# Hymba-style hybrid layer on 8 cores: q and k of the retention heads transposed by DMA, a dense state product, and another order of the weight loads

## The chip, the cores and the metric

The kernel runs on the 8 cores of one Trainium2 chip, one program on all of them with different data. The metric is device time in microseconds (us) of the slowest core. TensorE (PE) does the matrix products and can transpose through the identity; VectorE (DVE), ScalarE (ACT) and GpSimd (POOL) do the elementwise work; SyncE (SP) issues every DMA of this kernel, loads, stores and transposes, in one order.

## The reference, cut to what matters

One layer: RMSNorm, one input projection split in eight, an attention branch with a sliding window of 128 keys (8 query heads, 2 key heads of 64), a retention branch (4 heads, q and k of 64, v of 128), a SiLU gate on each, one output projection, the residual, a last RMSNorm. BATCH is 4, SEQ 8192, D_MODEL 1024. The retention part, which the change touches:

```python
q = rotate_pairs(q, cos, sin)
k = rotate_pairs(k, cos, sin) * (RET_QK_DIM ** -0.5)
...
sc = jnp.einsum('bnchd,bnmhd->bnhcm', q, k) * decay_in[None, None]
o_inner = jnp.einsum('bnhcm,bnmhe->bnche', sc, v)
kv_chunk = jnp.einsum('bnmhd,bnmhe,hm->bnhde', k, v, k_dec).astype(jnp.float32)
def step(state, kv):
    return state * chunk_decay[None, :, None, None] + kv, state
_, prev = lax.scan(step, init, jnp.moveaxis(kv_chunk, 1, 0))
...
o_cross = jnp.einsum('bnchd,bnhde,hc->bnche', q, prev, q_dec)
```

## The kernel before, in words

**Split.** Each core computes one half of one sequence: 32 main chunks of 128 tokens (32 to 63; `NP` is 32). Ahead of them it runs 32 prefix chunks (0 to 31), which only build the retention state that the half starts from. (For a first half they are zeros; the work is the same.)

**Prefix chunk.** x is loaded (512 KB, 7 slots `xs`), its norm computed (ACT squares and sums, L680, POOL takes the power, L683) and the rows scaled to `hh` (L524 on ACT or L526 on DVE). PE transposes `hh` (`st_T`, 8 matmuls, L701), DVE or ACT copies the result to `hT`, PE multiplies by the k columns of the weights (`st_P_prefix`, L708, 8 matmuls of 256 columns), DVE rotates a pair of chunks (`ev_rot`, L740, L743 and two adds), and PE adds k times `hh` to four banks (`st_G`, L948, 4 matmuls of 512 columns). In the same stretch the weights come in: `load_wr` loads 16 pieces of 640 KB through three staging slots `wstage`, and ACT and DVE cast them to bf16 in `Wa` (v, key, value, q and k columns) and `Wb` (attention q and the two gates). A piece of part 0 holds `Wa`'s columns and a first quarter of attention q's, one of part 1 the rest of `Wb`. Then `load_wo` brings the output weights, 8 pieces of 512 KB. A piece can be loaded only when the cast of the piece three before it is done.

**Main chunk.** `st_P_main` part 1 projects attention q, k and v, retention q and k (rotated to `qk` by `ev_rot`, four slots) and v; part 2 (`P2`) the two gates. `st_R` transposes `qk` on PE (4 transposes) into a bank and copies it out in three pieces, `kT` and two zero-padded `qTp`, padded so that two heads share a 128-row product. `st_SC` and `st_scT` make the two kinds of scores, `st_PV`, `st_OR` and `st_KV` the outputs and the new state `Sst`, `st_M` transposes the mixed output by DMA, `st_O` multiplies by the output weights `Wo`, adds x and norms, `st_store` stores.

**Order.** The stages are laid out over steps t by the list `order`: an entry ("name", offset in the prefix, offset in the main part) runs chunk t - offset. In a step of the main part the stages come as T (chunk t+1), load (t+3), tload (t+4), M (t-2), store (t-4), PV, OR and KV (t-1), O (t-3), R (t), SC (t), P (t+1), scT (t), P2 (t+1), front (t+3). PE and SP run strictly in this order. ACT, DVE and POOL get theirs from a planner (`Sched.schedule`) that simulates the five engines with estimated costs, 310 GB/s for DMA among them, and picks at each moment the most urgent ready operation; some copies may go to either of two engines. On the chip every engine then runs its list in order, with semaphores between them. Small constants go by `emit_late_consts` at step NP - 12, the 512 KB of final gains `fg_rep` with them, all on one semaphore that is waited for in full.

## Time and profile before

| | |
|---|---|
| time of 3 runs | median 671.64 us (670.05 to 704.31) |
| profiled execution | 673.29 us; its span on the slowest core 671.7 us |
| spans of the 8 cores | 661.8 to 671.7 us, granted clock 0.965 to 0.980 |
| PE busy | 607.1 us, 90% |
| DVE busy | 525.8 us, 78% |
| ACT busy | 414.8 us, 62% |
| POOL busy | 204.3 us, 30% |
| DMA | 50.4% of 16 engines' span, 94.14 MB |

The profile shows the slowest core. The time of an execution is 1.6 us more than that core's span. Busy shares are means over two parts: the prefix with the weight loads, until some 124 us, and the main chunks behind it. A slice's granted clock of 1.00 is TensorE at its 2.4 GHz level. In a timeline the duration of a row of PE has the filling of the array in it, so that the distance of two starts, and not a duration, says what an instruction costs.

### The profile page before, as it was taken

What the parts mean: (1) busy time and instruction counts of PE and PEld (TensorE: products, weight loads), DVE (VectorE), ACT (ScalarE), POOL (GpSimd) and SP (SyncE); (2) the same over time, 40 slices, a digit from 0 to 9 for tenths busy, and PEclk for the clock granted to TensorE, in tenths of its full rate; (3) what the DMA queues carried; (4) which work ended last, traced back from release to release, by engine and by line L of the source; (5) the groups of instructions that cost most, each with busy time, mean ns of one, the idle gap of its engine ahead of it and who ended that gap; (6) DMA issues with size and microseconds to landing.
All of it is one profiled execution on the core that took longest, in us unless ns stands there. A gap on an engine that the chain in (4) does not pass through costs nothing.

```text
span 671.7 us, 19097 instructions; the slowest of 8 cores (661.8 to 671.7 us)
## 1 busy us (share of the span) xinstructions
PE 607.1 (90%) x5059; PEld 372.0 (55%) x5059; DVE 525.8 (78%) x1047; ACT 414.8 (62%) x732; POOL 204.3 (30%) x264
## 2 busy tenths in 40 slices
PE   0697869797899999999999999999999999999974
PEld 0464646555555555566555556566555655555541
DVE  0687877556678888888888888788888888888874
ACT  4776877564446756766666567666676675665532
POOL 2644432212212323322322322323333332332230
PEclk9997879798899999999999999999999999999978
DMA  7999997723324444535625446637356353414113
GB/s 191 337 311 337 325 307 226 248 64 80 80 64 111 110 113 126 131 77 133 135 65 159 111 99 124 128 95 131 101 130 147 101 132 101 112 49 111 49 48 110
DMA packets 89337, 94.14 MB, mean 140 GB/s; under 512 B 68624, under 2 KB 69008, under 8 KB 89232
## 3 DMA queue, kind: packets, MB, share of 16 engines
q1 hardware_dynamic: 89232, 92.93, 50.4%
q8 instruction: 43, 0.70, 0.4%
q14 instruction: 62, 0.51, 0.3%
HBM read 59.88 MB, written 16.78 MB: 114 GB/s over the span
## 4 chain that ended last, share of the span: by engine, by line
PE 78%; DMA 5%; issue 5%; DVE 5%; ACT 4%; POOL 2%; SPq 1%; DVEq 0%; POOLq 0%; ACTq 0%
PE ps L708 34%; PE ps L1018 16%; PE ps L714 11%; PE ps L871 4%; PE ps L948 2%; PE ps L904 2%; DMA dkt<-dk_pre 2%; DMA fg_rep_s<-fg_rep 2%; PE ps L701 1%; DMA wstage<-w_o 1%; PE ps L994 1%; PE ps L990 1%; ACT PT L874 1%; PE ps L929 1%; PE ps L849 1%
## 5 line engine op out<-in xcount | busy, mean ns | idle before, releaser
L708 PE MATMUL ps<-Wa,hT 128*128 128x512 bf16 (+2 forms) x1032 | 169.5, 319 | 2.2 <-DVE hT L512 2.2
L708 PEld LDWEIGHTS ps<-Wa,hT 128*128 128x128 bf16 x1032 | 89.8, 100 | 59.9 <-issue 2.6
L708 PE MATMUL ps<-Wb,hT 128*128 128x512 bf16 x512 | 115.7, 379 | 1.9 <-ACT sqk L771 1.9
L1018 PE MATMUL ps<-Wo,mixT 128*128 128x512 bf16 x512 | 116.0, 380 | 0.0
L880 POOL TENSOR_SCALAR_AFFINE_SELECT PT<-PT 128x1024 bf16<-128x1024 bf16 x63 | 81.2, 1301 | 52.3 <-ACT PT L874 52.3
L1001 POOL TENSOR_TENSOR gns<-gns,neghalf 128x4 f32<-128x4 f32 x32 | 33.0, 1031 | 174.8 <-DVE gns L999 174.7
L1018 PEld LDWEIGHTS ps<-Wo,mixT 128*128 128x128 bf16 x512 | 50.3, 98 | 54.6 <-issue 1.0
L708 PEld LDWEIGHTS ps<-Wb,hT 128*128 128x128 bf16 x512 | 48.5, 98 | 56.1 <-issue 2.9
L874 ACT ACTIVATE PT<-ps,negC 128x1024 bf16<-128x1024 f32 x64 | 71.1, 1113 | 4.3 <-DVE negC L782 3.8
L680 ACT ACTIVATE junk<-xs 128x1025 bf16<-128x1025 f32 x64 | 67.5, 1055 | 2.7 <-DMA xs<-x_all 1.3
L714 PEld LDWEIGHTS ps<-hT,Wb 128*128 128x128 bf16 x1024 | 63.9, 102 | 5.7 <-issue 2.5
L714 PE MATMUL ps<-hT,Wb 128*128 128x128 bf16 x1024 | 66.7, 227 | 0.0
L683 POOL TENSOR_TENSOR stat<-stat,neghalf 128x1 f32<-128x1 f32 x64 | 41.6, 659 | 79.6 <-ACT junk L680 76.6
L510 ACT ACTIVATE kT<-ps 128x256 bf16<-128x256 bf16 x31 | 11.9, 383 | 85.6 <-PE ps L849 85.6
L831 ACT ACTIVATE gate<-ps 128x512 f32<-128x512 f32 x64 | 38.2, 596 | 42.9 <-PE ps L708 17.0
L834 DVE SCALAR_TENSOR_TENSOR gate<-gate,ps 128x512 f32<-128x512 f32 x64 | 43.8, 685 | 12.7 <-ACT gate L831 10.8
L1029 POOL TENSOR_TENSOR stat<-stat,neghalf 128x1 f32<-128x1 f32 x32 | 17.6, 550 | 112.2 <-ACT junk L1027 112.2
L1022 DVE TENSOR_TENSOR yy<-ps,xs 128x512 f32<-128x512 f32 x64 | 44.2, 691 | 4.7 <-PE ps L1018 1.6
L1031 DVE SCALAR_TENSOR_TENSOR yy<-yy,stat,fg_rep_s 128x1024 f32<-128x1024 f32 x32 | 40.9, 1277 | 7.9 <-POOL stat L1029 7.7
L871 PE MATMUL ps<-aqT,kTa 128*128 128x512 bf16 x128 | 35.5, 381 | 8.4 <-DVE Sst L937 4.7
L1027 ACT ACTIVATE junk<-yy 128x1025 bf16<-128x1025 f32 x32 | 33.9, 1060 | 13.9 <-DVE yy L1022 10.2
L740 DVE TENSOR_TENSOR rotu<-ps,tb 128x512 f32<-128x512 f32 x48 | 33.0, 687 | 6.7 <-PE ps L708 5.5
(126 smaller groups left out, 1009.3 us busy)
## 6 DMA issues: line engine op xcount, KB each, us to landing
xs<-x_all SPq DMA_DIRECT2D x64, 512.0 KB, 8.3
out<-yy SPq DMA_DIRECT2D x32, 512.0 KB, 3.1
wstage<-w_r SPq DMA_DIRECT2D x16, 640.0 KB, 11.5
tb<-tabs SPq DMA_DIRECT2D x32, 256.0 KB, 4.6
wstage<-w_o SPq DMA_DIRECT2D x8, 512.0 KB, 7.1
wstage<-w_k SPq DMA_DIRECT2D x2, 512.0 KB, 6.6
gate<-cs_pre SPq DMA_DIRECT2D x2, 512.0 KB, 13.0
fg_rep_s<-fg_rep SPq DMA_DIRECT2D x1, 512.0 KB, 11.5
```

The costliest lines, as they stand in the source:

```text
L680: S.add("act", lambda e: e.activation(out=junk[:, 0:D + 1], in_=xs[sx][:, 0:D + 1], func=AF.Square, accum_out=stat[st][:, 0:1]), reads=[b_ ...
L683: S.add("pool", lambda e: e.tensor_tensor(out=stat[st][:, 2:3], in0=stat[st][:, 0:1], in1=neghalf[:, 0:1], op=ALU.pow), reads=[b_stat[st], ...
L708: S.add("pe", lambda e, kb=kb: e.matmul(bank[:, c0:c0 + n], lhsT=hT[c % 2][:, kb * 128:(kb + 1) * 128], rhs=W[:, kb, w0:w0 + n], start=(kb ...
L714: S.add("pe", lambda e, kb=kb: e.matmul(bank[:, c0:c0 + 128], lhsT=W[:, kb, w0:w0 + 128], rhs=hT[c % 2][:, kb * 128:(kb + 1) * 128], start ...
L831: S.add("act", lambda e, bank=bank, gi=gi: e.activation(out=gate[s2][:, gi * 512:(gi + 1) * 512], in_=bank[:, 0:512], func=AF.Tanh, scale= ...
L834: S.add("dve", lambda e, bank=bank, gi=gi: e.scalar_tensor_tensor(out=gate[s2][:, gi * 512:(gi + 1) * 512], in0=gate[s2][:, gi * 512:(gi + ...
L871: S.add("pe", lambda e, bank=bank, sk=sk, g=g, first=first: e.matmul(bank[:, g * 512:(g + 1) * 512], lhsT=kTa[sk][g][:], rhs=aqT[s2][:], s ...
L874: S.add("act", lambda e, blk=blk, bank=bank: e.activation(out=PT[s2][blk][:], in_=bank, func=AF.Exp, bias=negC[s2][:, 0:1], scale=ATT_SCAL ...
L880: S.add("pool", lambda e, blk=blk, sgn=sgn, op=op: e.affine_select(out=PT[s2][blk][:], in_=PT[s2][blk][:], pattern=[[0, 8], [-sgn, 128]], ...
L1018: S.add("pe", lambda e, kb=kb, bank=bank, half=half: e.matmul(bank[:, 0:512], lhsT=mixT[s2][:, kb * 128:(kb + 1) * 128], rhs=Wo[:, kb, hal ...
L1022: S.add("dve", lambda e, bank=bank, half=half: e.tensor_tensor(out=yy[s2][:, half * 512:(half + 1) * 512], in0=bank[:, 0:512], in1=xs[sx][ ...
L1031: S.add("dve", lambda e: e.scalar_tensor_tensor(out=yy[s2][:, 0:D], in0=yy[s2][:, 0:D], scalar=st[:, 2:3], in1=fg_rep[:], op0=ALU.mult, op ...
```

## The change

Retention q and k are rotated straight into a zero-padded tile `qkp` of 8 blocks of 128 columns (two slots; in the prefix into the buffers `PT[1]`), and one DMA transpose makes all of `qkT` from it. The transposes on PE and the three copies are gone, and stage R moves ahead of M in the order. The state product takes the padded k: four products of 128 columns, accumulated in pairs, in place of two of 256, and the state is updated by two fused DVE operations in place of one multiply and two adds. `load_wr` loads 8 pieces of 640 KB, one per step `-4 + 22 i // 7`; the rest of attention q comes as two pieces of 512 KB at steps 19 and 21, the gates' columns as eight pieces of 512 KB at steps 24 to 31 with buffers of their own (`b_Wg`), the output weights four each at steps 32 and 33 (before: one each at steps 26 to 33), the constants at step 25 (before 20), and `fg_rep` by itself at step 34. The last x that the prefix's part of the order loads (chunk 33) is at step 24, chunk c at step c - 9.

```diff
-    order=[("T", None, -1), ("load", -9, -3), ("tload", -3, -4), ("M", None, 2), ("store", None, 4), ("GF", 2, None),
-           ("PV", None, 1), ("OR", None, 1), ("KV", None, 1), ("O", None, 3), ("G", 1, None), ("R", None, 0), ("SC", None, 0),
+    order=[("T", None, -1), ("load", -9, -3), ("tload", -3, -4), ("R", None, 0), ("M", None, 2), ("store", None, 4), ("GF", 2, None),
+           ("PV", None, 1), ("OR", None, 1), ("KV", None, 1), ("O", None, 3), ("G", 1, None), ("SC", None, 0),
...
+    qkp_all = sb("qkp", [128, 2 * 1024 + 128], BF16)
+    qkp = [qkp_all[:, i * 1024:(i + 1) * 1024] for i in range(2)]
+    qkT, b_qkT = slots("qkT", 2, [128, 8, 128], BF16)
+    qk_pre = [PT[1][i // 2][:, (i % 2) * 512:(i % 2 + 1) * 512] for i in range(4)]
...
+    S.add("pool", lambda e: e.memset(qkp_all[:], 0.0), writes=b_qk)
...
+    def emit_fg():
+        S.add("sp", dma(fg_rep[:, :], fg_d[:, :]), writes=[b_fgs], dmaq="fg")
...
+    def load_wq(half):
+        st_t, b_st, q = stage_slot()
+        S.add("sp", dma(st_t[:, 0:1024], wq_d[:, half * 1024:(half + 1) * 1024]), writes=[b_st], dmaq=q)
+        for i in range(4):
+            kb = half * 4 + i
+            cast(Wb[:, kb, 256:512], st_t[:, i * 256:(i + 1) * 256], g_col[:, kb:kb + 1], b_st, b_Wb[kb])
+    def load_wg(kb):
+        st_t, b_st, q = stage_slot()
+        S.add("sp", dma(st_t[:, 0:D], wg_d[kb * 128:(kb + 1) * 128, :]), writes=[b_st], dmaq=q)
+        cast(Wb[:, kb, 512:WB], st_t[:, 0:D], g_col[:, kb:kb + 1], b_st, b_Wg[kb])
...
-            cast(Wb[:, kb, 256:WB], st_t[:, :], col, b_st, b_Wb[kb])
...
-    for i in range(16):
-        w_tasks.setdefault(min(-4 + (30 * i) // 15, -4 + (i * (NP - 2)) // 15), []).append(
-            lambda i=i: load_wr(i // 2, i % 2))
     for i in range(8):
-        w_tasks.setdefault(NP - 6 + i, []).append(lambda i=i: load_wo(i))
+        task(-4 + (i * (NP - 10)) // 7, load_wr, i)
+    for i in range(2):
+        task(NP - 13 + 2 * i, load_wq, i)
+    for i in range(8):
+        task(NP - 8 + i, load_wg, i)
+    for i in range(8):
+        task(NP + i // 4, load_wo, i)
...
     def st_R(c):
-        for j in range(4):
-            S.add("pe", lambda e, j=j: e.transpose(pb[:, j * 128:(j + 1) * 128], qk[c % 4][:, j * 128:(j + 1) * 128],
-                                                   ident_bf[:]),
-                  reads=[b_qk[c % 4], b_const], writes=[bb])
-        S.add(cp(kT[s2][:].rearrange("p a b -> p (a b)"), pb[:, 256:512]), reads=[bb], writes=[b_kT[s2]])
-        for r in range(2):
-            S.add(cp(qTp[s2][r][r * 64:(r + 1) * 64, :, :].rearrange("p a b -> p (a b)"),
-                     pb[r * 64:(r + 1) * 64, 0:256]),
-                  reads=[bb], writes=[b_qTp[s2]])
+        S.add("sp", lambda e: e.dma_start_transpose(out=qkT[c % 2][:], in_=qkp[c % 2]),
+              reads=[b_qk[c % 2]], writes=[b_qkT[c % 2]], dmaq=f"tq{c % 2}", cost={"sp": 1.25, "dma": 4.0})
...
     def st_KV(c):
         for j in range(2):
-            S.add("pe", lambda e, j=j: e.matmul(bank[:, j * 256:(j + 1) * 256],
-                                                lhsT=qk[c % 4][:, 256 + j * 128:256 + (j + 1) * 128], rhs=rvv[:, j],
-                                                start=True, stop=True),
+            for r in range(2):
+                q = r * 2 + j
+                S.add("pe", lambda e, j=j, r=r, q=q: e.matmul(
+                    bank[:, j * 128:(j + 1) * 128], lhsT=qkp[c % 2][:, r * 512 + (2 + j) * 128:r * 512 + (3 + j) * 128],
+                    rhs=rv[c % 3][:, q * 128:(q + 1) * 128], start=(r == 0), stop=(r == 1)),
...
-        S.add(tt(Sst[:].rearrange("p a b -> p (a b)"), Sst[:].rearrange("p a b -> p (a b)"), cdtab[:], ALU.mult),
-        for r in range(2):
-            S.add("dve", lambda e, r=r: e.tensor_tensor(out=Sst[r * 64:(r + 1) * 64, :, :],
+        for j in range(2):
+            S.add("dve", lambda e, j=j: e.scalar_tensor_tensor(
+                out=Sst[:, j, :], in0=Sst[:, j, :], scalar=cdtab[:, j * 128:j * 128 + 1], in1=bank[:, j * 128:(j + 1) * 128],
+                op0=ALU.mult, op1=ALU.add), reads=[bb, b_S, b_constB], writes=[b_S])
...
-        if t == max(0, NP - 12):
+        if t == max(0, NP - 7):
             emit_late_consts()
+        if t == NP + 2:
+            emit_fg()
```

## Rows read from the trace of the kernel before

**Rows 1.** Busy time by stretch: start:end, length, PE, PEld, DVE, ACT, POOL, clock, DMA share, GB/s.

```profile
50.00:85.00 35.00, 28.53 (x220) 19.31 (x218) 29.12 (x51) 25.58 (x41) 16.06 (x23) 0.85 1.00 328
85.00:118.00 33.00, 26.21 (x216) 18.45 (x216) 24.43 (x48) 24.66 (x33) 10.46 (x16) 0.90 0.81 268
320.00:400.00 80.00, 79.46 (x683) 47.65 (x682) 67.59 (x142) 51.83 (x95) 24.33 (x25) 1.00 0.43 107
```

**Rows 2.** Timeline of PE in the prefix: start, us, line, operation, count, idle before.

```profile
15.39 1.01 PE L701 MATMUL ps<-ident_bf_s,hh 128*128 128x128 bf16 x8 [15.39 <-DVE hh L526]
...
68.45 0.61 PE L701 MATMUL ps<-ident_bf_s,hh 128*128 128x128 bf16 x8
...
70.64 0.61 PE L701 MATMUL ps<-ident_bf_s,PT 128*128 128x128 bf16 x8
...
93.52 1.01 PE L701 MATMUL ps<-ident_bf_s,hh 128*128 128x128 bf16 x8 [4.08 <-DVE hh L526]
...
115.25 0.61 PE L701 MATMUL ps<-ident_bf_s,hh 128*128 128x128 bf16 x8 [1.25 <-DVE hh L526]
...
121.43 0.27 PE L765 MATMUL ps<-sqk,ones_bf 128*128 128x128 bf16 x1 [3.65 <-ACT sqk L771]
...
124.06 3.16 PE L714 MATMUL ps<-hT,Wb 128*128 128x128 bf16 x32
```

**Rows 3.** Timeline of SP's DMA issues at the prefix's end.

```profile
93.46 1.82 SPq L497 DMA_DIRECT2D xs<-x_all  x2
...
100.53 9.91 SPq L497 DMA_DIRECT2D wstage<-w_o  x3
...
122.62 0.33 SPq L497 DMA_DIRECT2D wstage<-w_o  x1
```

**Rows 4.** Costliest groups by shape: count, busy us, mean ns, idle before it.

```profile
L510 ACT ACTIVATE qTp<-ps 64x256 bf16<-64x256 bf16 x60 | 22.7, 378 | 5.3 <-ACT qTp L510 0.7
L937 DVE TENSOR_TENSOR Sst<-Sst,ps 64x256 f32<-64x256 f32 x64 | 26.5, 415 | 2.6 <-DVE Sst L937 0.5
L512 DVE CAST kTa<-ps 64x128 bf16<-64x128 f32 x51 | 14.6, 286 | 16.9 <-PE ps L708 13.7 <-ACT kTa L510 1.9
```

**Rows 5.** Timeline of PE over two main chunks.

```profile
323.50 1.95 PE L714 MATMUL ps<-hT,Wb 128*128 128x128 bf16 x32
...
330.51 3.61 PE L708 MATMUL ps<-Wb,hT 128*128 128x512 bf16 x16 [0.27 <-ACT sqk L771]
...
339.70 1.95 PE L714 MATMUL ps<-hT,Wb 128*128 128x128 bf16 x32
...
350.72 0.38 PE L929 MATMUL ps<-rv,qk 128*128 128x256 bf16 x2
350.94 3.62 PE L1018 MATMUL ps<-Wo,mixT 128*128 128x512 bf16 x16
354.39 0.39 PE L849 MATMUL ps<-ident_bf_s,qk 128*128 128x128 bf16 x4
354.62 1.03 PE L871 MATMUL ps<-aqT,kTa 128*128 128x512 bf16 x4
355.48 1.95 PE L714 MATMUL ps<-hT,Wb 128*128 128x128 bf16 x32
...
361.83 0.39 PE L890 MATMUL ps<-qTp,kT 128*128 128x128 bf16 x4
```

**Rows 6.** What PE waited for from 200 to 600 us: total us, times, longest.

```profile
PE ps L708 <- ACT sqk L771: 1.9, 7, 0.3
```

**Rows 7.** Timeline of DVE: the second rotation add of a main chunk.

```profile
349.57 0.42 DVE L517 TENSOR_TENSOR qk<-rotw,rotu 128x256 bf16<-128x256 f32 x1
```

**Rows 8.** Timeline of SP: the transpose of the mixed output behind it.

```profile
351.53 1.22 SPq L691 DMA_TRANSPOSE mixT<-mix  x1
```

**Rows 9.** The transposes into `mixT`, from issue to landing.

```profile
DMA to landing us min/median/max: 3.0/3.4/6.0
```

**Rows 10.** DMA issues: tiles, queue, count, KB each, median us to landing.

```profile
wstage<-w_r SPq DMA_DIRECT2D x16, 640.0 KB, 11.5
```

95 lines of the change are left out of this document (47 added, 48 removed).

## The prediction

> **What bounds the kernel now.** I read the busy time by stretches first, then PE's and SP's timelines at the places where the stretches differ, then the groups by shape for durations, last the waits. From 320 to 400 us PE is busy for 79.46 of 80 us at the full clock, with DVE at 84% and ACT at 65% [rows 1]: the main chunks are bound by PE, and only what leaves PE's list shortens them. A chunk takes 15.78 us (339.70 to 355.48), or 16.20 where PE waits ahead of the gates (323.50 to 339.70) [rows 5].
>
> The prefix is another matter. PE is busy for 28.53 of 35 us from 50 to 85 us, at a clock of 0.85, while the 16 DMA engines are busy all the time at 328 GB/s [rows 1]. Counted from the transposes of chunk 0 at 15.39 us, those of chunk 32 come at 115.25, so that a chunk takes 3.12 us; where nothing is late it takes 2.19 (68.45 to 70.64) [rows 2]. So some 30 us of the prefix's 100 are not PE's work. Three candidates stand behind them: DMA, full until 85 us; DVE and ACT, together 103.8 us busy in the 68 us from 50 to 118, 76% of each [rows 1]; and single stalls, of which 93.52 (4.08 us idle) and 121.43 (3.65 us) are the largest [rows 2].
>
> **1. Fewer bytes ahead of the prefix's x.** By the order, and with 0.524 MB for a chunk of x or a 512 KB piece and 0.655 for 640 KB, what had to move before: x of chunks 0 to 30, 16.3 MB; 14 pieces of w_r, 9.2; k columns and tables, 2.2; constants with the gains, 1.05. That is 28.7 MB, 88 us at 0.328 MB per us [rows 1], behind some 3 us of start: 91 us, and SP does issue the next x at 93.46 [rows 3]. After the change: 16.3 of x, 8 pieces, 5.2, k columns and tables 2.2, the two pieces of attention q 1.05: 24.8 MB, 76 us, so 79. DMA brings the prefix's x 12 us earlier. Chunk 32 followed that issue by 22 us in the trace (93.46 to 115.25), since seven slots of x lie between; I keep this lag. The other bounds of this term: if DVE and ACT set the pace, it is almost nothing, since nearly all of their work stays (the gates' casts only move; two output weights' casts and the gains' scaling, about 3 us of ACT, leave). At two engines fully busy, their 103.8 us over 68 and a like share before need about 76 us for what takes 101 now, and PE needs 15.4 + 32 x 2.19 = 85.5 us at least: the gain cannot pass 22 us. I take 12, and 1 more for the 4.08 us stall, which ends a wait of DVE and POOL for the constants with the 512 KB of gains: the gains go by themselves now, but a wait for the rest stays. **-13 us**, ends -3 and -22.
>
> **2. The gap ahead of the first main chunk.** PE waits 3.65 us until 121.43 for ACT's square of the key [rows 2]; ACT there sits behind output weights that SP issues from 100.53 to 122.62 [rows 3]. They go away, but the gates' weights come to ACT just before in their place. **-2 us**, ends 0 and -3.65.
>
> **3. The gates' weights.** Eight pieces from step 24. Cumulated up to the last one: 24.8 MB, three more x, 1.6, eight pieces, 4.2, constants and tables, 1.6: 32.2 MB, 98 us, 101 with the start. Part 2 of chunk 32 needs them all. Part 2 starts 7 us behind part 1 (323.50 to 330.51) [rows 5]; with items 1 and 2 part 1 of chunk 32 starts at 109 in place of 124.06 [rows 2], part 2 at 116. So they are hidden by 15 us if DMA is the limit; cost 0. If they come at the pace of the output weights, one per 3.2 us (8 in 22 us, [rows 3]), issued from step 24 (about 84 us, where the x's of item 1 end) on, the last is issued at 107 and cast by 114: still hidden, by 2 us. This cover is thin, and it is a rival below.
>
> **4. Output weights and gains in the main part.** 4.7 MB at steps 32 to 34, first needed by O of chunk 32 three steps after. DMA is busy 43% in main chunks [rows 1], and 14 us of full DMA spread over some 50 us fit. But SP's list is strict: the transposes for chunks 33 (R) and 34 (hT) stand behind them, and casts of 1 to 2 us fall on ACT and POOL in the chunks that start the pipeline. **+1 us**, ends 0 and +4.
>
> **5. Four transposes less on PE.** From the first to the next instruction 0.23 us (354.39 to 354.62) [rows 5] for 32 chunks: **-7 us**. This is exact as long as PE is the bound; the lower end is -5, if the first and last chunks don't give it. The state product stays equal: two of 256 columns take 0.22 us (350.72 to 350.94), and four of 128 also take 0.22, as the four transposes show. The longer list of weight loads is hidden under the products, as now.
>
> **6. Relief of ACT and DVE.** ACT loses three copies of 0.38 us, 1.1 us per chunk; DVE loses the multiply and two adds (0.41 + 2 x 0.415, [rows 4]) and gets two fused operations on 128 x 128 from PSUM. The trace has none of these; a cast from PSUM of 128 columns takes 0.286, a 256-column add 0.415 [rows 4], and I take 0.29, the row of the same width: 1.24 less 0.58, so 0.66 us less per chunk. Neither engine is the bound; what it can return is the wait for ACT's sqk ahead of the gates, 7 times from 200 to 600 us [rows 6], each of which goes with a chunk of 16.20 instead of 15.78. Between 0 and -3 us: **-1.5**. The rotation's adds write the same number of elements in another stride: 0, ends 0 and +0.1 us of DVE a chunk, hidden. The one fill of `qkp` on POOL, some 2 us, lies in the start, where POOL waits.
>
> **7. R as a DMA transpose.** Its issue holds SP for 1.22 us as `mixT`'s does [rows 8], and it lands 3.0 to 6.0 us after, median 3.4 [rows 9]. It waits for the second rotation add, at 349.57 + 0.42 = 350.0 [rows 7]; its reader, the product of q and k, starts at 361.83 [rows 5]. 11.8 us against 3.4: hidden by 8. Queued behind R on SP are M (here issued at 351.53 [rows 8], so at most 1.3 us later, and its reader O one full chunk behind), the store, and the next step's T, load and tload, each read half a chunk or more later. DMA's share rises from 0.43 by some 0.1: x, tables and output are 1.31 MB a chunk, 4.0 us at the full rate, 0.25 of it, so that the two transposes now fill the other 0.18 and one more is 0.09. Cost 0, and what it costs if the cover goes is the rival below.
>
> On this point the Trainium skill speaks against the change: "VectorE: DVE Perf Modes", in its rules for kernel authors, says to transpose 128 x 128 on TensorE where a PSUM destination is fine, and by DMA otherwise; in "The three transpose paths" it gives 390 ns against 1309 ns. By an estimate from this page eight blocks one behind the other would take 10.5 us; that would still end at about 360.5, 1.3 us ahead of the reader, and the sum would be the same by a hair. The trace's 3.4 us for an equal tile decides it here.
>
> **Sum.** -13 - 2 + 0 + 1 - 7 - 1.5 + 0 = -22.5 us. The profiled execution takes 673.3 us (span 671.7), so 650.8; it lies 1.7 above the median of the runs, so **649 us** against 671.6. About 2% (13.4 us) is what a measurement of this kernel can tell from no change.
>
> **Rivals.** (a) The prefix doesn't speed up: DVE, ACT and the planner's order set its pace, for which it speaks that chunk 32 comes 22 us behind the issue of its x. Against it: both stand at 76%. Then -3 for item 1, and -1 - 7 - 1 of the rest: 660 us. Chance 0.17. (b) The gates' weights come late: three staging slots, casts in ACT's list, 2 us of cover. Late by 6 us, PE idles, and its clock falls as in the stretches with gaps (0.85 and 0.90 [rows 1]): 6 us and 1 for the clock, 656 us. Chance 0.13. (c) Slower: the new wait in SP's queue, or R's landing, decides. A 640 KB load took 11.5 us to land in the full prefix [rows 10]. From the point where a transpose needs more than 11.8 us from the last rotation add, each us costs 32; at 13 us, with 1.2 over, +38 against -22: 687 us. For it: three transposes in one queue. Against it: the DMA share of 0.43. Chance 0.06. (d) The order by the planner comes out worse in the main chunks, with waits of 0.4 us in each: 660 us. Chance 0.06. My forecast: 0.58.
>
> Faster by over 2% (below 658.2): the forecast, most of (b), a fourth of (a) and (d): 0.75. Slower by over 2%: 0.05. Within: 0.20. The range reaches from the forecast with item 1 near its far end (-9 more), item 2 and 6 at theirs (-3), 637, to (a) and (d) with some more, 664.
>
> **What would show it.** The transposes of chunk 32 near 102 us and PE's first main product near 109; DMA at full share for less than 80 us, then the gates' pieces until about 100; no transposes of `qk` on PE, chunks of 15.55 us, steady; `qkT` landing in 3 to 4 us and no wait of PE for it; DVE near 82% in main chunks. The forecast is wrong if chunk 32 stays near 112, if PE waits for a gate weight, or if main chunks stay at 15.8.

## The result and the profile after

The changed kernel takes 664.02 us (median of 4 runs, 662.81 to 664.97) against 671.96 for the kernel before beside it: a ratio of 0.989, with an interval of 0.987 to 0.992. The forecast was 649, range 637 to 664. The change is worth 8 us where 22.5 were expected; it is faster, by less than 2%. In some executions the cores of one die run several per cent slower (704.31 us in one of the four of the kernel before, more in a few below); every ratio and every range given here leaves those out. The profiled execution took 664.39 us, its span 662.8 on core 4.

The busy time by stretches comes first, as in [rows 1] (start:end, length, PE, PEld, DVE, ACT, POOL, granted clock, DMA share, GB/s):

```profile
50.00:85.00 35.00, 26.43 (x215) 18.23 (x213) 30.07 (x53) 28.44 (x48) 16.89 (x25) 0.90 0.95 318
85.00:118.00 33.00, 24.60 (x220) 17.32 (x219) 22.64 (x44) 24.55 (x34) 6.57 (x11) 0.90 0.89 276
320.00:400.00 80.00, 80.00 (x685) 47.63 (x684) 66.69 (x137) 48.41 (x85) 24.78 (x27) 1.00 0.55 146
```

The last line is the success: PE is busy 80.00 of 80 us, the waits of before are gone, and ACT and DVE have less to do. The first two hardly differ from before: PE is no busier between 50 and 118 us than it was (51.0 us against 54.7), though fewer bytes lie ahead of it. DMA's share is 0.95 where it was 1.00, and 0.89 where it was 0.81; DVE and ACT together are at 105.7 of 136 engine-microseconds.

PE's timeline in the prefix, the transposes of a chunk each (those of chunks 17, 18 and 32 are the rows at 63.65, 73.18 and 106.51):

```profile
15.02 1.01 PE L722 MATMUL ps<-ident_bf_s,hh 128*128 128x128 bf16 x8 [15.02 <-DVE hh L530]
...
63.65 0.61 PE L722 MATMUL ps<-ident_bf_s,hh 128*128 128x128 bf16 x8
...
69.81 1.86 PE L729 MATMUL ps<-Wa,hT 128*128 128x256 bf16 x8 [5.55 <-DVE hT L516]
...
73.18 1.06 PE L722 MATMUL ps<-ident_bf_s,PT 128*128 128x128 bf16 x8
...
102.14 0.61 PE L722 MATMUL ps<-ident_bf_s,mix 128*128 128x128 bf16 x8 [0.89 <-DVE mix L530]
...
106.51 0.61 PE L722 MATMUL ps<-ident_bf_s,hh 128*128 128x128 bf16 x8
...
116.19 0.27 PE L796 MATMUL ps<-sqk,ones_bf 128*128 128x128 bf16 x1 [7.30 <-ACT sqk L802]
```

Chunk 32 comes at 106.51 instead of 115.25 [rows 2], 8.7 us earlier, not 13. And the wait for ACT's square of the key, 3.65 us before, is now 7.30. The key is that of chunk 31, the last of the prefix, which the first main chunk's window needs; so this wait falls between the transposes of chunk 32 and its first product.

PE's timeline of a main chunk:

```profile
330.67 1.95 PE L735 MATMUL ps<-hT,Wb 128*128 128x128 bf16 x32
...
337.02 0.39 PE L911 MATMUL ps<-qkT 128*128 128x128 bf16 x4
...
341.69 0.39 PE L951 MATMUL ps<-rv,qkp 128*128 128x128 bf16 x4
341.91 3.62 PE L1035 MATMUL ps<-Wo,mixT 128*128 128x512 bf16 x16
345.36 1.03 PE L892 MATMUL ps<-aqT,kTa 128*128 128x512 bf16 x4
346.23 1.95 PE L735 MATMUL ps<-hT,Wb 128*128 128x128 bf16 x32
```

Start to start it is 346.23 - 330.67 = 15.56 us, against 15.78 in [rows 5]. The transposes ahead of L892 are gone, and the state product takes the 0.22 us (341.69 to 341.91) that were expected of four products of 128 columns.

To place the difference I read five marks on each of the 8 cores and take medians: the transposes of chunk 32 (T32), the first products of chunks 32, 36 and 63 in the main part (P32, P36, P63), and the end of the span.

| us | T32 | P32 | P32 to P36 | P36 to P63 | P63 to end | end |
|---|---|---|---|---|---|---|
| before | 112.8 | 121.7 | 69.6 | 431.9 | 45.2 | 668.3 |
| after | 104.8 | 117.0 | 69.4 | 421.0 | 51.3 | 658.7 |
| difference | -8.0 | -4.7 | -0.2 | -10.9 | +6.1 | -9.6 |

A column is the difference of two medians. By the slowest cores the change is worth 671.7 less 662.8, 8.9 us, and by the medians of the runs 7.9. So the forecast's 22.5 went three ways: 10.3 us are missing in the prefix (-4.7 for -15), 6.1 were lost at the end, where nothing was expected, and the main part gave 3.6 more than the 7.5 that items 4 to 6 sum to. -22.5 + 10.3 + 6.1 - 3.6 = -9.7. The experiments are about these three.

**Where in the prefix the 8.0 us came.** The same medians for more chunks' transposes, with the half of the change that keeps the old loads (below) beside them:

| us | T17 | T18 | T23 | T24 | T25 | T32 |
|---|---|---|---|---|---|---|
| before | 66.6 | 68.8 | 85.5 | 92.0 | 96.2 | 112.8 |
| old loads, R by DMA and dense product | 63.3 | 65.4 | 80.2 | 91.5 | 95.5 | 111.9 |
| after | 63.2 | 72.1 | 84.3 | 86.5 | 88.7 | 104.8 |

At chunk 23 the change had gained 1.2 us. Between chunks 23 and 25 it gained 6.3 more, behind chunk 25 the last 0.5. What lies between chunks 23 and 25 in the kernel before is the 4.08 us stop at 93.52 [rows 2]. DVE and POOL stand there until the constants have landed, the 512 KB of gains with them (DVE, then POOL, core 1):

```profile
91.13 0.17 DVE L569 TENSOR_SCALAR sinks<-sinks_s 128x8 f32<-128x8 f32 x1 [1.32 <-DMA fg_rep_s<-fg_rep]
...
91.97 2.71 POOL L683 TENSOR_TENSOR stat<-stat,neghalf 128x1 f32<-128x1 f32 x4 [2.97 <-DVE negsinkmax L573]
```

POOL's four powers are those that the scaling of the next chunks' rows waits for. In the kernel of the table's second row the prefix has come further by then, the stop is longer, and chunk 24 comes at the same time (core 6, DVE and PE):

```profile
90.71 0.17 DVE L569 TENSOR_SCALAR sinks<-sinks_s 128x8 f32<-128x8 f32 x1 [6.78 <-DMA fg_rep_s<-fg_rep]
...
93.10 1.01 PE L701 MATMUL ps<-ident_bf_s,hh 128*128 128x128 bf16 x8 [9.82 <-DVE hh L528]
```

So in the old order of loads the landing of the constants pinned chunk 24, and most of the prefix's gain is that wait gone. Whether the gains by themselves, the later step or the fewer bytes ahead took it away, no run separates. Against it stands a new stop, the 5.55 us at 69.81 above: chunk 18 comes 3.3 us later than before.

### The profile page after: what moved, and what is told of

Same layout as the page of the kernel before. It is cut to its first block, busy times and chain, and to the rows that moved or that the text cites. A ratio compares the mean times of both kernels' runs of the same rounds, so it can differ in the third digit from the quotient of the medians.

```text
span 662.8 us, 18824 instructions; the slowest of 8 cores (655.3 to 662.8 us)
## 1 busy us (share of the span) xinstructions
PE 594.6 (90%) x4995; PEld 362.1 (55%) x4995; DVE 503.1 (76%) x1001; ACT 384.6 (58%) x657; POOL 201.0 (30%) x262
## 4 chain that ended last, share of the span: by engine, by line
PE 79%; DMA 9%; DVE 3%; ACT 3%; issue 3%; POOL 1%; SPq 1%; DVEq 0%; POOLq 0%; ACTq 0%
PE ps L729 36%; PE ps L1035 16%; PE ps L735 11%; DMA xs<-x_all 5%; PE ps L892 4%; PE ps L925 2%; DMA wstage<-w_g 2%; PE ps L965 2%; DMA wstage<-w_r 1%; PE ps L911 1%; PE ps L1007 1%; PE ps L1011 1%; PE ps L951 1%; PE ps L789 1%; ACT junk L701 1%
## 5 line engine op out<-in xcount | busy, mean ns | idle before, releaser
L729 PE MATMUL ps<-Wa,hT 128*128 128x512 bf16 (+2 forms) x1032 | 165.6, 314 | 9.2 <-DVE hT L516 8.0
L729 PEld LDWEIGHTS ps<-Wa,hT 128*128 128x128 bf16 x1032 | 87.8, 99 | 66.1 <-issue 9.9
L729 PE MATMUL ps<-Wb,hT 128*128 128x512 bf16 x512 | 117.2, 383 | 0.0
L901 POOL TENSOR_SCALAR_AFFINE_SELECT PT<-PT 128x1024 bf16<-128x1024 bf16 x63 | 77.3, 1236 | 62.8 <-ACT PT L895 62.7
L701 ACT ACTIVATE junk<-xs 128x1025 bf16<-128x1025 f32 x64 | 67.6, 1056 | 10.5 <-DMA xs<-x_all 5.7
L514 ACT ACTIVATE Sbfp<-Sst 128x256 bf16<-128x256 f32 x31 | 12.9, 417 | 73.5 <-DVE Sst L956 70.5
L865 DVE SCALAR_TENSOR_TENSOR gate<-gate,ps 128x512 f32<-128x512 f32 x64 | 43.7, 684 | 10.5 <-ACT gate L862 8.3
L892 PE MATMUL ps<-aqT,kTa 128*128 128x512 bf16 x128 | 35.1, 388 | 8.6 <-DVE Sst L956 4.3
## 6 DMA issues: line engine op xcount, KB each, us to landing
wstage<-w_r SPq DMA_DIRECT2D x8, 640.0 KB, 12.3
```

Source lines behind the costliest of these rows:

```text
L701: S.add("act", lambda e: e.activation(out=junk[:, 0:D + 1], in_=xs[sx][:, 0:D + 1], func=AF.Square, accum_out=stat[st][:, 0:1]), reads=[b_ ...
L729: S.add("pe", lambda e, kb=kb: e.matmul(bank[:, c0:c0 + n], lhsT=hT[c % 2][:, kb * 128:(kb + 1) * 128], rhs=W[:, kb, w0:w0 + n], start=(kb ...
L865: S.add("dve", lambda e, bank=bank, gi=gi: e.scalar_tensor_tensor(out=gate[s2][:, gi * 512:(gi + 1) * 512], in0=gate[s2][:, gi * 512:(gi + ...
L892: S.add("pe", lambda e, bank=bank, sk=sk, g=g, first=first: e.matmul(bank[:, g * 512:(g + 1) * 512], lhsT=kTa[sk][g][:], rhs=aqT[s2][:], s ...
L901: S.add("pool", lambda e, blk=blk, sgn=sgn, op=op: e.affine_select(out=PT[s2][blk][:], in_=PT[s2][blk][:], pattern=[[0, 8], [-sgn, 128]], ...
```

## The experiments

Each was timed beside the kernel before in the same job; "marks" are the medians over cores, as above. A ratio is against the kernel before.

### Each half alone

The weights' half alone (the order and form of the loads; transposes and state product as before):

```
 kernel before
-    for i in range(16):  w_tasks ... load_wr(i // 2, i % 2)
-        w_tasks.setdefault(NP - 6 + i, []).append(lambda i=i: load_wo(i))
+    for i in range(8):   task(-4 + (i * (NP - 10)) // 7, load_wr, i)
+    for i in range(2):   task(NP - 13 + 2 * i, load_wq, i)
+    for i in range(8):   task(NP - 8 + i, load_wg, i)
+        task(NP + i // 4, load_wo, i)
+        if t == NP + 2:  emit_fg()
...
```

> The kernel before with the changed weight loads alone; R on TensorE and the old state product stay. Marks are medians over the 8 cores: before, chunk 32's transposes at 112.8 us, first main product at 121.7, chunk 63's first product at 623.2, end 668.4; changed kernel 104.8, 117.0, 607.4, 658.8. Theory A (the parts add, the prefix's gain is the weights'): first main product at 117, then the old 501.5 us to chunk 63 and the old tail of 45.2: some 667 us. Rival B (the tail's loss of 6.3 us comes from the weights and gains, loaded later): tail 51, 673 us.

Measured: 677.21 us (674.93 to 678.5) against 671.37, ratio 1.008 (1.006 to 1.011): slower. T32 105.9, P32 117.7, P36 to P63 436.2, end part 46.4. The prefix is shorter by 4 us, as in the whole change, and P36 to P63 is longer by 4.3.

The other half alone (R as a DMA transpose, `qkp`, dense state product; loads as before):

```
 kernel before
-            S.add("pe", lambda e, j=j: e.transpose(pb[:, j * 128:(j + 1) * 128], qk[c % 4][...], ident_bf[:]), ...)
-        S.add(cp(kT[s2]...)) ; for r in range(2): S.add(cp(qTp[s2][r]...))
+        S.add("sp", lambda e: e.dma_start_transpose(out=qkT[c % 2][:], in_=qkp[c % 2]), ...)
-        S.add(tt(Sst, Sst, cdtab, ALU.mult)) ; for r in range(2): add of a 64x256 half
+        for j in range(2): scalar_tensor_tensor(Sst[:, j, :], cdtab, bank, mult, add)
...
```

> The changed kernel's DMA transposes of q and k and its dense state product, with the weight loads of before. Theory A (the parts add, the tail's loss belongs to this part): first main product at 121.7 as before, chunk 63 some 490 us later, tail 51 in place of 45: 667 us. Rival B (the tail's loss is from the weight loads): tail 45, 661 us.

Measured: 665.13 us (665.04 to 665.39), ratio 0.991 (0.988 to 0.993). T32 111.9, P32 121.7, P36 to P63 422.9, end part 50.0. So the prefix's gain is the weights' half's but for 0.9 us at T32, none of which is left at P32, and the main part's gain is wholly this one. The halves don't add: +5.8 and -6.2 us alone, -8 together. Where the weights' half lost its time is seen on core 4 of that kernel, in PE's timeline at the start of one of the last chunks:

```profile
602.74 0.38 PE L892 MATMUL ps<-aqT,kTa 128*128 128x512 bf16 x1 [0.95 <-DVE gg L1024]
...
606.05 0.38 PE L892 MATMUL ps<-aqT,kTa 128*128 128x512 bf16 x1 [2.94 <-DVE Sst L958]
```

The chunks there are 20.0 and 17.4 us apart; all those from chunk 36 to 61 are at 15.8 to 16.7. No weight is loaded any more at 600 us. PE's list is the same, instruction by instruction, as in the kernel before (5059 in both traces), and so is SP's from 150 us on. What differs is the lists of DVE, ACT and POOL that the planner wrote; the second half of the state's add stands on DVE behind the 1.28 us of the final norm's product and its wait.

### The end of the kernel: R's place

```
 changed kernel
-    order=[..., ("tload", -3, -4), ("R", None, 0), ("M", None, 2), ("store", None, 4), ("GF", 2, None),
+    order=[..., ("tload", -3, -4), ("M", None, 2), ("store", None, 4), ("R", None, 0), ("GF", 2, None),
```

> The changed kernel with one entry moved: stage R comes behind M and store in the order, in place of ahead of them. Theory A (ahead of M, R's place in SP's list hands its urgency to the rotation, and the shift of the attention's exponent, negC, falls behind it on DVE, which costs only where PE's list runs out): tail 46 to 47 us in place of 51.4, time 659 to 660. Rival C (the fused state update makes the tail longer): tail 51, time 664.

Measured: 659.49 us (658.51 to 661.29), ratio 0.982 (0.979 to 0.986), 4.5 us less than the change as it is. P32 117.5, P36 to P63 422.8, end part 45.3 in place of 51.3. What PE waited for from 600 us on (total us, times, longest), first the changed kernel, then this one:

```profile
PE ps L911 <- ACT PT L895: 4.7, 2, 2.4
PE ps L892 <- DVE Sst L956: 4.3, 1, 4.3
PE ps L925 <- POOL PT L901: 0.7, 1, 0.7
PE ps L1035 <- DMA mixT<-mix: 0.4, 1, 0.4
```

```profile
PE ps L911 <- ACT PT L895: 2.4, 1, 2.4
PE ps L892 <- DVE Sst L956: 2.2, 2, 1.7
PE ps L925 <- POOL PT L901: 0.7, 1, 0.7
```

One wait for the exponential, 2.24 us on core 4, is gone and that for the state is halved (the rows are of core 4 and of core 7, the slowest of each). The first of them begins far from PE. DVE in the changed kernel (start, us):

```profile
606.79 0.16 DVE L808 TENSOR_TENSOR tmpc<-Mk 128x1 f32<-128x1 f32 x1
...
618.15 0.15 DVE L811 TENSOR_TENSOR tmpc<-tmpc,Mq 128x1 f32<-128x1 f32 x1
...
618.68 0.27 DVE L813 TENSOR_SCALAR negC<-tmpc,cst,negsinkmax 128x1 f32<-128x1 f32 x1
```

The small operation that closes the softmax's bound stands 11 us behind its partner. What it reads had been there since 606.79; the list puts the final norm's product of a finished chunk (1.28 us) and the next chunk's rotation ahead of it. So ACT's exponential can start only at 619.10, and PE stands still at 620.36. After each such stop PE runs at the lower level for a while: from 612 to 640 us PE is busy for 18.39 of 28 us at a granted clock of 0.83 here, and for 22.65 at 0.88 with R behind. R's own data were in time: it landed 3.0 to 5.0 us after its issue, median 3.1, and PE never waited for it. R's place isn't the only edit that shortens the end. The runs below that change nothing but the prefix or the loads have an end part of 46.5 to 47.7 us too, so that the row of stops is shown as read in the trace, and R's place as its cause is not.

### The casts of the gates' weights allowed on POOL

```
 changed kernel
-        S.add(alts, reads=[st_buf, b_gs] + ([b_gnc] if gn else []), writes=[b_dst])
+        S.add(alts, reads=[st_buf, b_gs] + ([b_gnc] if gn is True else []), writes=[b_dst])
-        cast(Wb[:, kb, 512:WB], ..., b_Wg[kb])
+        cast(Wb[:, kb, 512:WB], ..., b_Wg[kb], "pool")
```

> The changed kernel with the casts of the gates' weights allowed on POOL beside ACT. Theory A (the 7 us wait ahead of the first main product is ACT, held in its list by casts that wait for the gates' loads): the stretch from chunk 32's transposes to the first main product falls from 12.3 us to 8 or 9, time 660 to 661. Rival D (the loads themselves set it): 12 us, time 664.

Measured: 656.58 us (656.01 to 656.92), ratio 0.978 (0.976 to 0.980). T32 105.1, P32 115.8: the gap is 10.7 us in place of 12.2, and not 8 or 9. The edit only allows POOL, and the planner sent two of the eight casts there:

```profile
L601 POOL TENSOR_TENSOR Wb<-wstage,g_col_s x2: 1892/1893/1894, 88.3 to 97.5; 128x1024 bf16<-128x1024 f32 x2
```

Six stayed on ACT, so the theory had a weak test. The end part is 47.6, 3.7 less, and that has no mechanism in this edit: its lists were planned anew. With R behind as well:

```
 changed kernel
+    both edits above
```

> Both edits that helped: R behind M and store, and the gates' casts on POOL or ACT. If they add: first main product at 116 us, tail 45, time 653 to 654. If wg_pool's shorter tail (47.6) was already the same gain as r_behind's: 655 to 656.

Measured: 657.23 us (656.06 to 657.52), ratio 0.978 (0.977 to 0.980): the same as the casts' edit alone. P32 115.6, end part 46.7. The two gains of the end part don't add.

### The fused update of the state

```
 changed kernel
+            S.add("dve", ... tensor_tensor(out=Sst, in0=Sst, in1=cdtab, op=ALU.mult))
-            ... scalar_tensor_tensor(out=Sst[:, j, :], ..., op0=ALU.mult, op1=ALU.add)
+            ... tensor_tensor(out=Sst[:, j, :], in0=Sst[:, j, :], in1=bank[...], op=ALU.add)
```

> The changed kernel with the state updated by a multiply and two adds of 128 columns in place of two fused operations; the dense product stays. DVE has some 0.4 us more per main chunk. Theory A (the tail's loss came with R's place): tail 50 to 52 us as in the changed kernel, main part 421, time 664 to 665. Theory C (the fused update made the tail longer): tail 46, time 659.

Measured: 663.06 us (661.45 to 663.43), ratio 0.986 (0.985 to 0.988); P36 to P63 421.2, end part 49.8. So the fusing as such is worth nothing that can be seen. In the changed kernel it takes

```profile
L956 DVE SCALAR_TENSOR_TENSOR Sst<-Sst,cdtab_s,ps x64: 293/340/349, 156.2 to 646.3; 128x128 f32<-128x128 f32 x64
```

340 ns in the median and not the 290 of my estimate.

### What limits the prefix

Three runs leave work out in the prefix. All three have their lists planned anew, and each is a single run. In the first the loads of five of the eight pieces of `w_r`, of `w_q` and of `w_g` are left out, the casts staying:

```
 changed kernel
-        S.add("sp", dma(st_t[:, 0:1024], wq_d[...]), ...)
-        S.add("sp", dma(st_t[:, 0:D], wg_d[...]), ...)
+        if kb < 3:
             S.add("sp", dma(st_t[:, :], wr_d[...]), ...)
```

> The changed kernel that leaves out the loads of five of the eight pieces of w_r, of the two of attention q and of the eight of the gates (8.5 MB); all their casts are still made, from what lies in the staging slots. Theory E (ACT and DVE): chunk 24's transposes at 84 to 86 us, chunk 32's at 103 to 105, first main product 5 us or more behind as the casts wait for nothing (110). Theory F (the loads): the 9 us step from chunk 17 to 18 falls to 3, chunk 24 at 78 to 80, chunk 32 at 96, first main product at 102 to 104.

In the second the prefix's squares go over 129 instead of 1025 columns:

```
 changed kernel
+        n0 = 0 if is_main(c) else 896
-        ... activation(out=junk[:, 0:D + 1], in_=xs[sx][:, 0:D + 1], func=AF.Square, ...
+        ... activation(out=junk[:, n0:D + 1], in_=xs[sx][:, n0:D + 1], func=AF.Square, scale=..., ...
```

> The changed kernel whose prefix chunks sum the squares over 128 columns of x (and the constant) in place of 1024: it leaves out 7/8 of that sum, some 0.8 us of ACT per prefix chunk. Marks as before, medians over the cores; changed kernel: transposes of chunk 17 at 63.1 us, of 18 at 72.1, of 24 at 86.5, of 32 at 104.8, first main product at 117.0. Theory E (ACT and DVE set the prefix's pace): chunk 24 some 8 us earlier, at 78, and chunk 32 at 96 to 99. Theory F (the loads' landing sets it, the full DMA): chunk 24 at 85 to 87, chunk 32 at 104.

And then both edits together:

> The changed kernel without the loads of five pieces of w_r, of w_q and of w_g (their casts stay and read what lies in the buffers), and with the prefix's squares taken over 129 of 1025 columns: both edits of the earlier runs nodma and cheap_sq together. Each alone left chunk 32's prefix transposes at 105 to 106 us. Theory A (the prefix after 50 us has two limits close to one another, the DMA engines with the in-order wait for their weights, and the work of ACT and DVE; each hides what the other one loses): together chunk 32's transposes are at 95 to 98, P32 at 106 to 109, the run 645 to 649 us. Theory B (neither of the two pins the prefix, but the chain per chunk, transposes, hT copy, products, rotation, state products, or DVE alone, which has 14 to 16 us of work in 20 in every variant): 102 or later, P32 at 112 or later.

| us | T18 | T24 | T25 | T28 | T30 | T32 | P32 | run |
|---|---|---|---|---|---|---|---|---|
| after | 72.1 | 86.5 | 88.7 | 95.3 | 100.5 | 104.8 | 117.0 | 664.02 |
| without the loads | 64.9 | 81.9 | 84.7 | 96.3 | 100.7 | 105.0 | 115.1 | 656.99 (one) |
| short squares | 61.1 | 81.2 | 83.5 | 90.1 | 100.2 | 105.0 | 115.2 | 655.24 (one) |
| both | 62.9 | 76.8 | 79.6 | 87.1 | 92.9 | 97.2 | 107.9 | 648.72 (one) |

Either edit alone brings chunks 18 and 24 forward by 5 to 11 us and chunk 32 not at all; both together bring chunk 32 forward by 7.6. That sum fits theory A of the third run; of the first two runs neither theory has both marks, T24 and T32. The busy times of core 0 from 65 to 85 us, without the loads, with the short squares, with both:

```profile
65.00:85.00 20.00, 16.53 (x143) 11.31 (x142) 19.55 (x36) 18.50 (x26) 9.51 (x13) 1.00 0.71 192
```

```profile
65.00:85.00 20.00, 16.16 (x131) 11.17 (x132) 17.43 (x31) 12.74 (x32) 10.47 (x16) 0.91 1.01 323
```

```profile
65.00:85.00 20.00, 18.59 (x169) 13.21 (x167) 19.70 (x39) 17.64 (x33) 9.57 (x13) 1.00 0.71 204
```

With the loads gone, DVE is busy 19.55 and ACT 18.50 of 20 us, with DMA at 0.71: this stretch is then bound by the two vector engines. With ACT relieved, DMA stands at its full share. With both lifted PE is busy 18.59 of 20.

The lead over the changed kernel is lost only behind these 20 us, and there no engine is full. Without the loads and with the short squares, core 0 from 85 us on:

```profile
85.00:105.00 20.00, 16.64 (x127) 11.50 (x126) 15.47 (x31) 17.63 (x26) 4.64 (x7) 0.83 0.29 82
```

```profile
85.00:105.00 20.00, 16.57 (x126) 11.54 (x125) 13.91 (x27) 11.90 (x18) 3.44 (x6) 0.83 0.84 277
```

Each has a stop of PE in it, with the granted clock at 0.83 over the stretch. Without the loads PE waits 3.36 us at 89.37 for a copy of `hT` that stands in ACT's list behind casts; the three chunks from 25 to 28 take 11.6 us. With the short squares it is the constants again, this time at step 25 (POOL, then PE):

```profile
93.95 2.71 POOL L705 TENSOR_TENSOR stat<-stat,neghalf 128x1 f32<-128x1 f32 x4 [8.77 <-DVE gn_col_s L579]
...
95.50 1.01 PE L723 MATMUL ps<-ident_bf_s,mix 128*128 128x128 bf16 x8 [3.43 <-DVE mix L530]
```

Every core has this stop, of 3.4 to 4.2 us, and the two chunks from 28 to 30 take 10.1 us; 5.2 us of lead end there. So that both edits together reach 97.2 and neither alone does is no proof of two limits of the whole prefix: one stop in each plan ate the lead. How much of the 7.6 us is the plan is open; `wo_late` below moves T32 by 6.8 us the other way with no edit to the prefix's work.

From the loads' side, SP's issue of the x of chunks 31 and 32 in the changed kernel:

```profile
81.30 2.89 SPq L501 DMA_DIRECT2D xs<-x_all  x2
```

In the kernel before, the x of chunk 31 was issued at 93.46 [rows 3]. That is 12.2 us earlier now, and the forecast's count of bytes gave 12, in part by luck: SP was waiting there not for the queue but for the slot of chunk 24's x, which came free only behind the stop for the constants (SP's longest wait between 80 and 96 us in the kernel before):

```profile
SPq L338 <- DVE hh L526: 7.3, 1, 7.3
```

The x before that, of chunk 30, was issued only 2.9 us earlier (82.23 to 79.32), that of chunk 32 11.1 (94.95 to 83.86). By landing they came 10.1 and 11.8 us earlier, so the transfers did gain about what the bytes say. It didn't help: in the changed kernel the x of chunk 32 landed at 89.75, and its transposes start at 106.51, 16.8 us later (13.7 in the kernel before). The lag from the issue of chunk 31's x to T32 grew from 21.8 to 25.2 us (81.30 to 106.51).

### The gap ahead of the first main product

The chain of the end goes through it like this in the changed kernel (start, us, what):

```profile
92.35 7.21 DMA wstage<-w_g
...
102.26 7.99 DMA wstage<-w_g
...
112.29 1.14 ACT Wb L600
...
114.48 0.84 issue
115.32 0.19 ACT junk L701
115.51 0.18 ACT Vaug L514
...
115.77 0.29 ACT sqk L802
```

Between 85 and 120 us 43.4% of the chain is the landing of gates' weights. The product that reads them is not what waits; ACT's list is, since their casts stand in it ahead of the square of chunk 31's key, which PE finished the products for at about 109 us. In the next run the gates' loads and casts are replaced by fills on POOL (the gates are then computed from zeros):

```
 changed kernel, load_wg(kb)
-        st_t, b_st, q = stage_slot()
-        S.add("sp", dma(st_t[:, 0:D], wg_d[...]), ...)
-        cast(Wb[:, kb, 512:WB], ...)
+        S.add("pool", lambda e: e.memset(Wb[:, kb, 512:WB], 0.0), writes=[b_Wg[kb]])
```

> The changed kernel with the eight loads and ACT casts of the gates' weights replaced by POOL memsets of the same tiles (the gates are then computed from zeros; the main part's instructions are all there). Theory A (the gates' loads and casts are what the prefix's end and the gap wait for, as the waits of ACT in front of sqk show): chunk 32's transposes are at 102 to 103 instead of 104.8, the gap to the first main product is 8 us instead of 12.2, P32 110 to 112. Theory B (the gap is the first main chunk's own chain and the output weights step into the place of the gates' weights): P32 stays at 115 to 117.

Measured: one run, 661.21 us. T32 106.9, P32 118.2, the gap 11.3: no gain at P32, and 0.9 us of the gap. ACT's waits from 95 to 120 us on core 0 hold this line,

```profile
ACT Wo L597 <- DMA wstage<-w_o: 2.5, 1, 2.5
```

and PE's wait for sqk is 5.5 us. The output weights, next in the list, have stepped into the place in part; ACT also waits 8.2 us for DVE, POOL and PE in these 25. So the chain above shows what held ACT in the changed kernel, and not that the gap would be shorter without it. (T18 is at 69.5, 2.6 earlier, yet T24 at 88.8, 2.3 later.) Moving those one chunk further, together with the casts allowed on POOL:

```
 changed kernel with the casts of the gates' weights allowed on POOL
-        task(NP + i // 4, load_wo, i)
+        task(NP + 1 + i // 4, load_wo, i)
```

> wg_pool (656.6 us) with the output weights' eight loads issued one chunk later. Theory A (in every variant the end of the prefix is pinned by ACT's list, in which casts that wait for whatever weights come last stand ahead of the squares of q and k of the first main chunk): the gap from chunk 32's transposes to its first product falls from 10.7 us to 7 to 8 us, P32 is 112 to 113, and the total 653 to 654 if the main part doesn't give it back. Theory B (the gap is the chain of the first main chunk itself, products, square, norm, rotation and transposes, with no previous chunk to fill it): P32 and the gap stay within 1 us, and the total at 656 to 658; if PE then waits for an output weight in chunk 32's last product, the start (P36 minus P32, 69.2) grows by 1 to 3.

Measured: 667.95 us (10 runs, 666.09 to 670.87), ratio 0.995 (0.993 to 0.997), 11 us slower than without the edit. T17 is already at 68.3 instead of 63.1, T32 at 111.9, P32 at 122.7, the gap 10.7: loads after chunk 32 were moved, and chunk 17 came 5 us later. The edit didn't test what it was meant to; the planner wrote another prefix, with all eight casts of the gates' weights on ACT. What the gap would be without output weights in it stays open.

### The planner's own figures

The planner orders the lists by costs that it is given. Four runs change one such figure and no stage; the order on DVE, ACT and POOL changes, and which of two engines makes a copy. The cost of a DMA transpose:

```
 changed kernel
-   cost={"sp": 1.25, "dma": 4.0}
+   cost={"sp": 1.23, "dma": 3.2}
```

> The changed kernel with one figure of the planner's cost model altered (a DMA transpose is costed at 1.23 us of SP's time and 3.2 us of landing instead of 1.25 and 4.0). The program issues the same instructions on the same data; PE's and SP's orders stay the same, and DVE's, ACT's and POOL's orders, and some choices between DVE and ACT, come out differently. Theory A (what the change was worth lies in its mechanisms, the planner's order being about as good either way): 664 us within 2. Theory B (differences of several us between variants, such as w_only's 5.8 us of loss and the 5 to 6 us by which R's place and the casts' engine shorten the tail, are mostly the planner's order of the vector engines in the main part and the tail): it differs from 664 us by 3 us or more, in main or tail, while the last prefix transposes stay at 105 and the first main product at 117.

Measured: 667.44 us (666.38 to 668.26), ratio 0.993 (0.992 to 0.995), 3.4 us slower than the change as it is. PE's and SP's lists are the same instructions in the same order. T32 104.5 and P32 116.5 stay, P36 to P63 421.2 stays; P32 to P36 is 73.7 instead of 69.4. A figure nearer to the measured 1.23 and 3.1 us made the start of the main part worse by 4.3 us, by the lists of DVE, ACT and POOL alone.

And the time from a load's end on the queue to its data:

```
 changed kernel with the casts of the gates' weights allowed on POOL
-                op.t1 = dma_free + 1.0
+                op.t1 = dma_free + 4.0
```

> wg_pool (the changed kernel with the casts of the gates' weights on POOL alone, 656.6 us) with the planner's assumed latency of a load raised from 1 to 4 us, so that DVE's and ACT's weight instructions stand later in their lists. Theory A (the 9 us step from chunk 17's to chunk 18's prefix transposes comes from DVE's list, in which the sum over the last piece of w_r stands ahead of chunk 17's hT copy and waits for a load that lands 9.6 us after its issue): the step shrinks to 5 us or less, chunk 24's transposes are at 82 to 84 instead of 86.5. Whether that reaches the first main product (115.8 in wg_pool) depends on the second wait, at ACT, for the gates' and the output weights: if that pins it, P32 stays at 115 to 116 and the total at 656 to 657; if the first stall counts, P32 is 112 and the total 652 to 653. Theory B (the DMA engines, busy 95%, are the limit of the prefix and the list only shows where it waits): nothing of the prefix moves by more than 1 us.

Measured: 653.53 us (653.19 to 654.63), ratio 0.973 (0.972 to 0.975), 3 us less than with the figure at 1 us, and the fastest that keeps the computation. One of the eight casts is on POOL here, not two and not all as the text above has it. And it wasn't by the way expected: the step from chunk 17 to 18 is still 8.3 us (64.1 to 72.4), T24 is at 87.5, later by 1, T32 at 106.2. DVE doesn't wait there for `w_r` any more and the copy of `hT` still stands behind its sum:

```profile
68.49 0.67 DVE L630 TENSOR_REDUCE vmean<-wstage 128x4 f32<-128x512 f32 x1
...
70.41 0.68 DVE L516 COPY hT<-ps 128x1024 bf16<-128x1024 bf16 x1
```

so there the place in the list, not the load, makes the stop (rows of core 0; in the changed kernel too DVE waits only 0.68 us for the load, while PE stands 5.55). The gain is in the gap, 8.5 us instead of 10.7, and the main part (-0.6) and the end (-0.8). The same figure in the kernel before, and with R behind as well:

```
 kernel before ; changed kernel with the casts allowed on POOL and R behind
-                op.t1 = dma_free + 1.0
+                op.t1 = dma_free + 4.0
```

> The kernel before with the planner's assumed latency of a load raised from 1 to 4 us and nothing else. Theory A (the assumed latency matters where weight casts wait in ACT's and DVE's lists, which the kernel before has as much of as the changed one): 667 to 670 us against 672, the gain in the gap ahead of the first main product (8.9 us). Theory B (the gain belongs to the changed loads at the prefix's end): 671 to 674, or slower, as the planner's own mark for the first main product moves 2.5 us later.

> lat4 (653.5 us: casts of the gates' weights on POOL, planner's latency of a load 4 us instead of 1) with R's transposes behind M's and the stores in the planner's list, as in r_behind. Theory A (the tail's gain of r_behind, 6 us, is independent of the rest): 648 us. Theory B (lat4's tail, 46.8 us, is already the short one of 45 to 47 that r_behind, wg_pool and combo have, so there is nothing more to gain, and the order differs by chance): 652 to 656.

Measured for the kernel before: 671.57 us against 670.85, ratio 1.0005 (0.999 to 1.002), no difference; P32 118.2 is 3.5 us earlier, but P36 to P63 is 434.0 and the end part 46.5, with steps of 19.7 and 17.4 us to its last two chunks, of the kind that the weights' half has. (T23 is 5.0 us earlier, 80.5, and T24 at 91.9 as before: the constants once more.) For the other: 655.47 us, ratio 0.976 (0.974 to 0.978), 2 us above the figure alone.

Last, the weights' half with the casts of the gates' weights allowed on POOL (two of eight moved):

```
 weights' half alone
+   the edit of the casts, as above
```

> w_only (the weights' part of the change alone, 677.2 us, main part 436.2 us against 431.9 of the kernel before) with the casts of the gates' weights on POOL alone; PE's and SP's orders are those of w_only. Theory A (the weights' part is a gain of 4 us in the prefix, and w_only's loss in the main part comes from the planner's order there, not from the weights): the main part is 430 to 433, and the total 667 to 670. Theory B (the loss in the main part belongs to the order of the loads that the weights' part brings, or to PE's order, which is unchanged here): main stays at 435 or more, and the total at 674 to 677.

Measured: 675.91 us (675.06 to 676.81), ratio 1.006 (1.005 to 1.008). P36 to P63 435.4, with 19.7 and 17.4 us for the last two steps. DVE's, ACT's and POOL's lists are new, PE's and SP's are not, and the loss stays. Yet it isn't PE's and SP's lists that make it: PE's is the same in the kernel before, and the kernel before has these steps too under another figure of the planner, with PE's and SP's lists unchanged. Of four plans of the three vector engines over the same list of PE one, that of the kernel before, is without the two long steps (17.0 and 15.8 there).

## Why the prediction was wrong

**Item 1, -13 us: the step that failed.** T32 came 8.0 us earlier, but not by this item's sum. Its 12 us were to come from fewer bytes ahead of the x. At chunk 23 they had brought 1.2. What failed is "Chunk 32 followed that issue by 22 us ...; I keep this lag". The issue at 93.46 was itself held 7.3 us by the stop for the constants, so it was no measure of the bytes; and the lag is work and waits of DVE, ACT, POOL and PE, not a delay of the transfer: x of chunk 32 lay 13.7 us before its transposes and lies 16.8 us now. The other term, 1 us for the 4.08 us stop, was mis-sized the other way: with the slower chunk behind it the stop cost 6.3 us from chunk 23 to 25, and nearly all of that came back. The item's bound for the case that DVE and ACT set the pace was "almost nothing"; for the bytes alone that is near what was measured. The 76% at which the two stood in [rows 1] was taken for room; without the loads they fill 38.05 of 40 engine-microseconds between 65 and 85 us.

**Item 2, -2 us: wrong in sign.** The gap from T32 to P32 grew from 8.9 to 12.2 us. The item did name what stands in the chain there ("the gates' weights come to ACT just before in their place"), and priced it at no more than the whole gain. That they made the gap longer is read from the chain; with their loads and casts gone it was still 11.3 us, so what it is due to, beyond ACT's list, stays open. **Item 3** is the same fault seen from the other side: the cover of the gates' weights was measured up to their reader, part 2 of chunk 32, and PE never waited for a gate weight. The cast's place in ACT's list wasn't priced. A cast that waits for its load holds everything behind it on its engine; here that is the square of chunk 31's key, which PE wants before the first product of chunk 32. Rival (b) had the right cause with the wrong victim; rival (a), 660 us, comes nearest in number, but in part by luck: its 4 us up to P32 stand against 4.7 measured, which are 8.0 less 3.3, and its 8 for the main part against 11.1, with 6.1 lost at an end that it doesn't have.

**Item 4, +1 us: about right.** P32 to P36 is 69.4 us against 69.6, but other items shorten this stretch. Like with like, the new loads add 1.9 us to it beside R by DMA (67.5 to 69.4) and 0.4 us in the kernel before (69.6 to 70.0), within what a plan alone can move.

**Item 5, -7 us: right.** 0.22 us a chunk, the 0.23 of the forecast to a hundredth, over 27 chunks from P36 to P63 5.9 us.

**Item 6, -1.5 us: right mechanism, size too small.** From P36 to P63 the kernel before takes 431.9 us, 27 times 15.78 are 426.1: 5.8 us of waits. After, 421.0 less 27 times 15.56 is 0.9. So 4.9 us came back, past the far end of -3, which counted only the wait for sqk in 400 us [rows 6] and left the rest of the stretch out. DVE lost 22.7 us of busy time (525.8 to 503.1) and ACT 30.2 (414.8 to 384.6), about as estimated; with the fusing undone the time stays, so ACT's copies, the moved order and the plan are what is left as a cause, which no run separates.

**Item 7, 0 us: right.** R is issued and landed as `mixT`'s transposes are:

```profile
L876 SPq DMA_TRANSPOSE qkT<-qkp x32: 1231/1232/2302, 128.0 to 619.3; - x32
...
DMA to landing us min/median/max: 3.0/3.1/5.0
```

PE has no wait for `qkT` from 200 us to the end, and rival (c) is out. The Trainium skill's preference for TensorE in "VectorE: DVE Perf Modes", rules for kernel authors, doesn't hold here as a choice of time: a transpose of 128 x 1024 holds SP for 1.23 us and lands 3.1 us after, and the half of the change with this transpose in it is the half that gains (ratio 0.991 alone), because PE is the bound and SP isn't. Its figure of 1309 ns for one 128 x 128 block isn't borne out for eight of them one behind the other (10.5 us by an estimate from that page).

**The end, 0 us: not in the forecast at all, +6.1 measured.** Rival (d) looked for a worse order in the main chunks; it came in the last two, where there is no next chunk to fill PE. It isn't the price of the change: R's place takes 6.0 us of it back, leave for the gates' casts to run on POOL 3.7, and edits to the prefix alone about as much. With the casts allowed on POOL, PE's and SP's lists are those of the change as it is; so the 3.7 us are the plan of DVE, ACT and POOL alone. Why the plan comes out so is open.

What stays open: which instruction's place makes the long last steps of the weights' half (the state's add in the rows above is read, not tested), which part of the edit took away the wait for the constants, and how long the gap ahead of P32 would be with no weight casts in ACT's list. The interval of a ratio says nothing of the spread between plans.

## What to carry to other kernels

Before a gain is booked for bytes taken off a full DMA queue, look whether the data wait in their buffers for the engines: here x lay there for 14 us, so that its earlier landing could bring little. Mark every chunk, not only the last: a single stop, for constants that are needed much later, can pin all that comes behind it whatever the pace ahead, and is worth more than its own length. A load is late for everything that stands behind its cast on the same engine, not only for the operation that reads the weight. Where a planner writes the lists, time two or three plans of the same change before a difference of under 1% is put down to the change.
